# Stick-breaking attention: later key tiles summed by VectorE, one minus-ones product per key tile on TensorE

## What is computed

```python
def stick_breaking_attention(q, k, v):          # s = 512, h = 4, d = 64
    scale = d ** -0.5
    kpos = jnp.arange(s)
    def block(i):                                # 128 queries
        z = jnp.einsum('bqhd,bkhd->bhqk', qb, k).astype(jnp.float32) * scale
        strict = kpos[None, :] < qpos[:, None]
        log_beta = jax.nn.log_sigmoid(z)
        log_rem = jnp.where(strict, jax.nn.log_sigmoid(-z), 0.0)
        suffix = lax.cumsum(log_rem, axis=3, reverse=True) - log_rem
        a = jnp.where(strict, jnp.exp(log_beta + suffix), 0.0).astype(v.dtype)
        return jnp.einsum('bhqk,bkhd->bqhd', a, v)
```

## Time and profile before

| | |
|---|---|
| median of 3 runs | 3446.58 us (3440.33, 3446.58, 3448.2) |
| span of the profiled execution | 3442.4 us |
| TensorE busy | 97% of the span |
| VectorE busy | 48% |
| ScalarE busy | 36% |
| GpSimd busy | 7% |
| DMA | mean 84 GB/s |

### The profile page before, as it was taken

How to read it: one execution, slowest core, us unless ns; L and a number is a source line. 1 busy time by engine, 2 the same in 40 slices (tenths; PEclk the granted TensorE clock), 3 DMA queues, 4 the chain that set the end, 5 groups by cost and what they waited for, 6 DMA issues and landing times. The chain is left out here.

```text
span 3442.4 us, 42159 instructions
## 1 busy us (share of the span) xinstructions
PE 3355.2 (97%) x15712; PEld 2626.8 (76%) x15716; DVE 1669.0 (48%) x2158; ACT 1222.1 (36%) x1831; POOL 238.6 (7%) x268
## 2 busy tenths in 40 slices
PE   8999999999999999999999999999999999999998
PEld 6667888775688877888775688887888776678887
DVE  6755443666444344443636554435443544654433
ACT  4343122432522233332444443324233344543233
POOL 1200000011000000000103300002000101300000
PEclk9999999999999999999999999999999989999999
DMA  6213322221243232332220133333332321023332
GB/s 169 63 48 86 97 98 97 86 80 49 73 103 95 98 104 73 97 98 98 75 64 25 38 103 97 97 98 94 96 94 97 86 74 32 20 86 98 97 98 67
DMA packets 434263, 288.19 MB, mean 84 GB/s; under 512 B 44529, under 2 KB 412317, under 8 KB 433897
## 3 DMA queue, kind: packets, MB, share of 16 engines
q1 hardware_dynamic: 431272, 280.02, 28.1%
q0 software_dynamic: 2736, 4.58, 0.9%
q10 hardware_dynamic: 144, 2.10, 0.2%
HBM read 284.53 MB, written 2.13 MB: 83 GB/s over the span
## 5 line engine op out<-in xcount | busy, mean ns | idle before, releaser
L2022 PE MATMUL bank<-hh,whi 128*128 128x512 f32 x2768 | 1093.3, 395 | 16.2 <-DVE hl L1470 7.2
L2023 PE MATMUL bank<-hl,whi 128*128 128x512 f32 x2768 | 1080.1, 390 | 0.0
L2024 PE MATMUL bank<-hh,wlo 128*128 128x512 f32 x2768 | 1079.9, 390 | 0.0
L1404 DVE TENSOR_TENSOR wlo<-raw,whi 128x1024 fp32r<-128x1024 f32 (+2 forms) x534 | 646.4, 1212 | 312.4 <-ACT whi L945 298.0
L945 ACT ACTIVATE whi<-raw 128x1024 fp32r<-128x1024 f32 (+2 forms) x534 | 546.4, 1034 | 258.3 <-PE bank L2024 257.9
L2022 PEld LDWEIGHTS bank<-hh,whi 128*128 128x128 f32 x2768 | 521.4, 188 | 150.3 <-issue 33.0
L2024 PEld LDWEIGHTS bank<-hh,wlo 128*128 128x128 f32 x2768 | 521.1, 188 | 109.4
L2023 PEld LDWEIGHTS bank<-hl,whi 128*128 128x128 f32 x2768 | 521.2, 188 | 108.3 <-issue 2.6
L2022 PE MATMUL bank<-fshi,whi 128*128 128x512 f32 (+1 forms) x1358 | 526.3, 388 | 3.6 <-ACT G L1090 1.6
L2023 PE MATMUL bank<-fslo,whi 128*128 128x512 f32 (+1 forms) x1358 | 522.6, 385 | 0.0
L2024 PE MATMUL bank<-fshi,wlo 128*128 128x512 f32 (+1 forms) x1358 | 522.5, 385 | 0.0
(11 more groups left out here) (257 smaller groups left out, 2565.9 us busy)
## 6 DMA issues: line engine op xcount, KB each, us to landing
raw<-in_ffn_w_gate SPq DMA_DIRECT2D x88, 512.0 KB, 3.8
raw<-in_ffn_w_up SPq DMA_DIRECT2D x88, 512.0 KB, 3.8
raw<-in_ffn_w_down SPq DMA_DIRECT2D x88, 512.0 KB, 3.5
raw<-in_w_in SPq DMA_DIRECT2D x78, 512.0 KB, 3.9
raw<-in_w_up SPq DMA_DIRECT2D x64, 512.0 KB, 4.0
raw<-in_w_down SPq DMA_DIRECT2D x64, 512.0 KB, 3.4
raw<-in_w_out SPq DMA_DIRECT2D x16, 512.0 KB, 4.0
raw<-in_w_in SPq DMA_DIRECT2D x18, 256.0 KB, 3.4
```

The source lines that it names most:

```text
L1404: dve.tensor_tensor(slot3(wlo, s, m), slot3(raw, s, m), slot3(whi, s, m).bitcast(F32), ALU.subtract).then_inc(c.lo_done.sem, 1)
L2022: pe.matmul(o, wh, ah, start=start, stop=False)
L2023: pe.matmul(o, wh, al, start=False, stop=False)
L2024: return pe.matmul(o, wl, ah, start=False, stop=stop)
```

## The change

VectorE keeps, in place, a running sum of the later tiles. A new step `z_acc` adds tile `jt + 1` (which by then holds the sum of all later ones) onto tile `jt`, once the `suf` of that tile has read it. It stands twice per pair, after the second and the third step. `suf` then needs one product with `minus` instead of up to three. A semaphore `sb_acc` orders the two engines. The four added items also make the list of stick steps longer, and so shift it against `fill`.

```diff
@@ plan
         if s:
             stick_steps.append(("suf_exp", s - 1))
+        if s % QT in (2, 3):
+            stick_steps.append(("z_acc", s - 1))
         if s < n_stick:
             stick_steps.append(("z_dve", s))
@@ signals
+            c.sb_acc = signal("sb_acc", 0, SB_H // 2 * (QT - 2))
@@ VectorE
+                    elif s[0] == "z_acc":
+                        p, jt, _ = stick_step(s[1])
+                        dve.wait_ge(c.sb_suf.sem, c.sb_suf.at(l, s[1] + 1))
+                        if jt == 1:
+                            dve.wait_ge(c.sb_acc.sem, c.sb_acc.at(l, (QT - 2) * p + 1))
+                        later = stick_tile(B_SP, jt)[:, :, P:S - P * jt]
+                        dve.tensor_tensor(later, later, stick_tile(B_SP, jt + 1), ALU.add).then_inc(c.sb_acc.sem, 1)
@@ TensorE
                         n = S - P * jt
+                        if jt < QT - 2:
+                            pe.wait_ge(c.sb_acc.sem, c.sb_acc.at(l, (QT - 2) * (p + 1) - jt))
                         pe.wait_ge(c.sb_sp.sem, c.sb_sp.at(l, s[1] + 1))
                         for head in range(2):
                             ins = pe.matmul(bank[:, zb + head, 0:n], tri, stick_tile(B_SP, jt)[:, head, :], start=False, stop=jt == QT - 1, skip_group_check=True)
-                            for j2 in range(jt + 1, QT):
-                                ins = pe.matmul(bank[:, zb + head, P * (j2 - jt):n], minus, stick_tile(B_SP, j2)[:, head, :], start=False,
-                                                stop=j2 == QT - 1, skip_group_check=True)
+                            if jt < QT - 1:
+                                ins = pe.matmul(bank[:, zb + head, P:n], minus, stick_tile(B_SP, jt + 1)[:, head, :], start=False, stop=True, skip_group_check=True)
```

## The result

| | before | after |
|---|---|---|
| median of 4 runs each | 3445.11 us (3440.33 to 3448.2) | 3460.72 us (3455.88 to 3463.88) |
| ratio | | 1.0048, 95% interval 1.0034 to 1.0062 |
| span of the profiled execution | 3442.4 us | 3462.1 us |
| mean granted clock of TensorE | 0.993 | 0.988 |

The change makes the kernel slower by 0.48%, some 16 us, with 7 us of products taken off TensorE. The forecast was +5.7 us with a range up to 3458 us.

A forecast was written before the change was run, and what follows sets the result against it. The prediction took TensorE, busy 97% of the span, as the bound. Net waits of +2.6 us and clock falls of +3.1 us gave +5.7 us, from the 3446.6 us median to 3452.3 us, range 3443.5 to 3458 us.

The forecast's parts named there:

- 6.96 us of products: TensorE's products at steps 2 and 3 of each pair that go, 3.48 us per layer, claimed as saved.
- The adds free: Eight VectorE adds, 0.42 to 0.69 us each, claimed hidden except 0.42 us in the chain at step 2.
- The waits: TensorE's idle places in the new order: 6.2 us of new waits per layer against 4.9 us saved.
- The sum of +2.6 us: Waits less savings over both layers: +0.35 us first pair and +0.95 us second pair, 1.30 us per layer.
- a fall: A stretch with TensorE at 1.2 instead of 2.4 GHz; one was claimed to cost 1.57 us.
- the long wait: TensorE idle before the suf of step 7: 3.73 us claimed, with a fall in both layers, +3.1 us.
- the first pair: Waits of 0.62 and 2.32 us where 2.05 us was; falls counted as before, one in two.
- the clock falls more often: Rival: two to three more falls, also at the first pair and behind the compress groups, +8.8 to +10.4 us; chance 0.20.
- The saving arrives: Rival: the new waits do not come, 9.8 us saved, 3436.8 us; chance 0.10.
- its point of decision: The saving arrives once the new waits of a layer stay under 1.4 us; the prediction had 6.2 us.

The follow-up runs named there:

- e8: e1 with the removed products still made, in the same shapes, into a free bank that nothing reads; 3445.08 us, ratio 1.0.
- e1: The changed kernel with its step list woven in the order of before and z_acc put in afterwards; 3441.18 us, ratio 0.9996.
- e2: The kernel before, all its products and no adds, in the changed kernel's order by four dropped placeholders; 3459.56 us, ratio 1.0045.
- e6: The changed kernel with unread matmuls only in the first pair: 8 before the suf of step 2, 4 before step 4's scores; 3453.08 us.
- e5: The changed kernel with 13 unread matmuls only in the wait before the suf of step 7; 3456.37 us, ratio 1.0038.
- e4: e1 with ScalarE's z_act moved right behind its z and suf_exp right behind its suf; 3428.44 us, ratio 0.9962.
- e12: The kernel before (three products, no adds) with only ScalarE's functions moved forward; 3435.53 us, ratio 0.9974.
- e3: The changed kernel with unread matmuls in its new waits: 8 before the suf of step 2, 4 before step 4's scores, 13 before step 7's suf; 3442.66 us.
- e9: e1 with four unread 512-column matmuls in front of each compress group; 3436.54 us, ratio 0.9975.
- e7: e1 with unread matmuls in its two waits, 7 before the 512-wide scores and 5 before the suf of step 7; 3441.45 us, ratio 0.9991.
- e11: The changed kernel with four unread 512-column matmuls in front of each compress group; 3461.01 us, ratio 1.004.

## Why the prediction was wrong in size

**The work.** 6.96 us of products: right. The 48 instructions are gone, and e8 against e1 puts back 7.5 us, 6.4 us once the two groups of runs are set level, with the wait before step 7 shorter by 0.9 us in all. The adds free: right in the old order (e8), and 0.42 us each at step 2 in the new one, in the chain as said (e2).

**The waits.** Right, to 0.2 us each. The sum of +2.6 us is +1.8 us with the measured waits, and by the split the work of the changed kernel is 2.4 us above before (3419.6 against 3417.2). That the order does it and not the work is shown by e2, which is as slow without any of the new work. What carried this part of the prediction was to walk the three engines through the new order instead of counting what the diff removes.

**The clock.** This is the step that failed. The prediction has it as "I count a fall for it in both layers: +3.1 us" for the long wait, and "I count it as before, one fall in two" for the first pair. Measured, the lost clock grew by 15.3 us in the runs and 18.2 us in the profiled section, where the sum had 3.1 us. A fall did come at the 3.3 us wait in both layers, as forecast, and the price of 1.57 us for 3.4 us at half clock was right; the number and the length of the falls were not. Three things were missing.
- The waits of the first pair were put at no change. They are worth 10.5 us (e6), against 4.3 us for the last wait (e5).
- A fall was taken for one stretch of 3.4 us. In the changed kernel two stretches of layer 0 last 10.2 us, and the one at the long wait 6.8 us in both layers. The rows of before held such a one, and the prediction used it only for a rival.
- The removal of products was taken to leave the clock alone. It goes with 4 us more lost clock in the old order (e1 against e8) and 6 us in the new one (after against e2, with few runs), though with none once ScalarE is early (e4 against e12).

Of the rivals, "the clock falls more often" was the right one, given 0.20 and at most three falls more than the forecast's two. Its +8.8 to +10.4 us were still too low. "The saving arrives" needed 9.8 us from work alone; its point of decision was right, the new waits of a layer came to 5.8 us (2.15, 1.00 and 2.64).

**The rule of the Trainium skill** (page "TensorE: Matmul & The Clock Gate", section "What's actually happening": half rate is the default, and activity releases it) pointed the right way, and e3 agrees with it, 18.2 us of lost clock back with matmuls that do nothing. In e1 the clock fell after 12.6 us in which TensorE's row had no gap and stayed low for 10.2 us more of the same, and four matmuls of 512 columns per compress group took 10.7 us of lost clock away (e9). So a row that is busy in the profile does not say that the clock is full, and the prediction's search for idle time alone could not find these falls.

**What stays open.** The profiled executions show which falls each fill removed (e3, e7, e9, e11), one execution each. Why the stretch at `c00` and `c01` goes with the first pair's waits filled (e6) and stays with the groups filled (e11) is not shown; that short idle time and groups of 64-column matmuls close together bring more time at half clock than either alone is a guess. Why the removed products cost clock in two orders and not in the third is open as well. How the falls of a run depend on where the execution starts was not tried either; the runs of the kernel before differ by 13 us among themselves (3438.8 to 3451.9).

## What to carry to other kernels

Where a scheduler weaves lists by their length, adding one item moves all others: print the new order of each engine and walk the chain across the engines before counting what the edit saves, and pin the order if only the work is to change. On a kernel bound by TensorE, split every run into lost clock and the rest; a few microseconds of idle time, or a group of matmuls with few columns, can cost more in clock than in waiting (here 18.2 us for 11 us of filled waits), and it may be a group without any gap. The cheap gain here was neither product nor add, but to let ScalarE take the links of the chain as soon as they are due: 8 us on the kernel before (e12), and 15 us together with the change (e4), which in that order is worth the 5 to 7 us that it was meant to bring.

## What the runs showed of the hardware

- The clock fell while TensorE's own row was busy without a gap: 10.2 us at 0.50 in e1, around groups of 64-column matmuls, behind 12.6 us at 1.00 without a gap.
- It fell inside waits of 1.00, 2.15 and 3.33 us (after, layer 0; in layer 1 inside the long one and within 0.8 us behind the other two), but behind only one of two waits of 2.05 us (before).
- Matmuls that nothing reads made a kernel faster: 25 per layer took 18 us off the changed kernel (e3), 16 per layer 4.6 us off e1 (e9).
- With 7 us of products removed the clock took back some 4 us in one order (e1 against e8) and nothing in another (e4 against e12).
